# FFN up-projection: three 256-column products into the same PSUM columns in place of a 512- and a 256-column one, with no copy and addition behind them

## The reference, cut to what matters

```
u = rms_norm_2(h, norm2_gain[l])
up = causal_depthwise_conv(u @ ffn_up_w[l].astype(dt), ffn_conv_w[l], ffn_conv_b[l])
a_branch, v_branch = jnp.split(up, 2, axis=-1)
h = h + (jax.nn.gelu(a_branch) * v_branch) @ ffn_down_w[l].astype(dt)
```

## Time and profile before

| what | us |
|---|---|
| median of 3 runs | 1531.29 |
| lowest and highest run | 1531.23, 1532.5 |
| span of the profiled execution | 1529.9 |
| TensorE busy in that span | 1484.0 |
| up stage, tiles 3 to 47 | 127.25 |

### The profile page before, as it was taken

The page is one execution under the profiler, slowest core; times in us unless marked ns, Lnnn a source line. Parts: engine busy times, 40 slices in busy tenths (PEclk is TensorE's granted clock), DMA queues, the critical chain, the costliest instruction groups (busy, mean ns, idle before and its releaser), DMA issues.

```text
span 1529.9 us, 19087 instructions
## 1 busy us (share of the span) xinstructions
PE 1484.0 (97%) x7702; PEld 877.0 (57%) x7702; DVE 544.2 (36%) x1133; ACT 456.5 (30%) x796; POOL 151.6 (10%) x124
## 2 busy tenths in 40 slices
PE   8989999999999999999999999999999999999998
PEld 6755454544444445974554544445444696788886
DVE  5645111121111113034311111211111577688965
ACT  4541111111111112453111111111111561577654
POOL 0211000000000002952100000000000530001200
PEclk9999999999999999999999999999999999999999
DMA  8655999999999999745699999999999765555410
GB/s 298 247 221 220 379 425 429 426 428 427 428 427 429 426 423 398 257 177 228 253 422 420 428 428 428 426 428 428 427 428 410 283 220 205 181 200 186 166 55 28
DMA packets 76227, 502.67 MB, mean 329 GB/s; under 512 B 4720, under 2 KB 6000, under 8 KB 49136
## 3 DMA queue, kind: packets, MB, share of 16 engines
q1 hardware_dynamic: 75280, 495.18, 79.5%
q0 software_dynamic: 864, 6.29, 1.0%
HBM read 500.40 MB, written 1.05 MB: 328 GB/s over the span
## 4 chain that ended last, share of the span: by engine, by line
PE 86%; DMA 5%; DVE 4%; ACT 2%; issue 2%; SPq 1%; POOL 1%; DVEq 0%; ACTq 0%
PE bank L969 26%; PE bank L1002 14%; PE bank L828 9%; PE bank L915 7%; PE bank L1283 6%; PE bank L793 5%; DMA ring<-in_w_up 4%; PE bank L1311 4%; PE bank L929 3%; PE bank L1285 3%; SPq L576 1%; PE bank L984 1%; PE bank L875 1%; PE bank L862 1%; PE bank L887 1%
## 5 line engine op out<-in xcount | busy, mean ns | idle before, releaser
L969 PE MATMUL bank<-ring,arena 128*64 128x512 f32 x1280 | 283.7, 599 | 8.5 <-issue 6.8
L969 PEld LDWEIGHTS bank<-ring,arena 128*64 128x64 f32 x1280 | 94.3, 138 | 192.8 <-issue 192.0
L969 PE MATMUL bank<-arena 128*64 128x512 f32 x576 | 169.9, 599 | 5.2 <-issue 5.2
L1906 DVE TENSOR_TENSOR arena<-arena,bank 128x512 f32<-128x512 f32 x32 | 22.0, 687 | 382.3 <-PE bank L969 382.3
L1002 PE MATMUL bank<-ring,arena 128*64 128x512 f32 x640 | 141.8, 595 | 2.4 <-ACT arena L1450 2.4
L1283 PE MATMUL bank<-x_split,w_high 128*128 128x512 f32 (+1 forms) x408 | 139.1, 393 | 0.2 <-DVE x_split L1731 0.2
L915 PEld LDWEIGHTS bank<-SEL,x_by_row 128*128 128x128 f32 x1024 | 116.7, 192 | 25.8 <-issue 24.3
L915 PE MATMUL bank<-SEL,x_by_row 128*128 128x128 f32 x1024 | 122.8, 278 | 0.0
L969 PEld LDWEIGHTS bank<-arena 128*64 128x64 f32 x576 | 55.9, 138 | 113.6 <-issue 113.6
L1920 DVE SCALAR_TENSOR_TENSOR y_low<-bank,ST,y_high 128x512 fp32r<-128x512 f32 x64 | 48.0, 751 | 202.4 <-ACT y_high L1454 202.4
L1454 ACT ACTIVATE y_high<-bank,ST 128x512 fp32r<-128x512 f32 x64 | 44.0, 687 | 245.6 <-PE bank L1002 245.6
(11 more groups left out here) (327 smaller groups left out, 2220.5 us busy)
## 6 DMA issues: line engine op xcount, KB each, us to landing
ring<-in_w_gate SPq DMA_DIRECT2D x32, 2048.0 KB, 27.5
ring<-in_w_up SPq DMA_DIRECT2D x32, 2048.0 KB, 23.0
ring<-in_w_down SPq DMA_DIRECT2D x32, 2048.0 KB, 24.5
arena<-in_w_gate SPq DMA_DIRECT2D x18, 2048.0 KB, 25.0
arena<-in_w_up SPq DMA_DIRECT2D x18, 2048.0 KB, 24.4
arena<-in_w_down SPq DMA_DIRECT2D x18, 2048.0 KB, 26.7
ring<-in_ffn_up SPq DMA_DIRECT2D x12, 2048.0 KB, 8.1
ring<-in_w_in SPq DMA_DIRECT2D x8, 2048.0 KB, 13.5
```

Of the source, the lines that this page charges most:

```text
L969: last = nc.tensor.matmul(bank[4 + m][64 * e:64 * e + 64, :], XG[:, c, 64 * e:64 * e + 64], w[e][:, c, :], start=(c == 0), stop=(c == C - 1))
```

## The change

For tiles 3 to 47 each of the 8 steps now issues three matmuls of 256 columns, all into the bank's columns `[0:256]`: `WHI` by `XHI`, `WHI` by `XLO`, `WLO` by `XHI`. The bank then holds the finished sum. For these tiles ScalarE's copy, VectorE's addition and their semaphore steps are gone; ScalarE's first tap and VectorE's other two read the bank itself through `up_sum(f)`. TensorE, before it writes a bank again, waits for the last tap of tile `f - 4` (`f_cv`, `ffn_conv`), where it waited for the addition (`f_sum`). Tiles 0 to 2 stay as they were.

```
-        FSUM = [cut(13312 + 256 * i, SEQ) for i in range(4)]
+        FSUM = [cut(13312 + 256 * i, SEQ) for i in range(WBUF)]
+
+        def up_sum(f):
+            return FSUM[f] if f < WBUF else bank[f % 4][:, 0:SEQ]
...
                 if f >= 4:
-                    pe.wait_ge(f_sum, f - 3)
-                up(f, 0, SEQ).then_inc(w_used, 1)
+                    pe.wait_ge(f_cv, f - 3)
+                w_high, w_low = WHI[f % WBUF], WLO[f % WBUF]
+                for c in range(C):
+                    for n, (a, b) in enumerate(((w_high, XHI), (w_high, XLO), (w_low, XHI))):
+                        last = nc.tensor.matmul(bank[f % 4][:, 0:SEQ], a[:, c, :], b[:, c, :],
+                                                start=(c == 0 and n == 0), stop=(c == C - 1 and n == 2))
+                last.then_inc(w_used, 1)
...
                     act.wait_ge(w_used, U_FFN + f + 1)
-                    if f >= 4:
-                        act.wait_ge(f_cv, f - 3)
-                    nc.scalar.copy(FSUM[f % 4], bank[f % 4][:, 0:SEQ]).then_inc(f_low, 1)
+                    if f < WBUF:
+                        nc.scalar.copy(FSUM[f], bank[f][:, 0:SEQ]).then_inc(f_low, 1)
                     high_weights(f + WBUF)
-                    act.wait_ge(f_sum, f + 1)
+                    if f < WBUF:
+                        act.wait_ge(f_sum, f + 1)
...
-                    nc.scalar.activation(CV[f % 4], FSUM[f % 4], ACT.Identity,
+                    nc.scalar.activation(CV[f % 4], up_sum(f), ACT.Identity,
...
             for f in range(FF2_T):
-                dve.wait_ge(f_low, f + 1)
-                v.tensor_tensor(FSUM[f % 4], bank[f % 4][:, SEQ:2 * SEQ], FSUM[f % 4], ALU.add).then_inc(f_sum, 1)
+                if f < WBUF:
+                    dve.wait_ge(f_low, f + 1)
+                    v.tensor_tensor(FSUM[f], bank[f][:, SEQ:2 * SEQ], FSUM[f], ALU.add).then_inc(f_sum, 1)
                 low_weights(f + WBUF)
...
-                    ins = v.scalar_tensor_tensor(CV[f % 4][:, j:SEQ], FSUM[f % 4][:, 0:SEQ - j], wj, CV[f % 4][:, j:SEQ],
+                    ins = v.scalar_tensor_tensor(CV[f % 4][:, j:SEQ], up_sum(f)[:, 0:SEQ - j], wj, CV[f % 4][:, j:SEQ],
                                                  ALU.mult, ALU.add)
```

## The result

| | before | after |
|---|---|---|
| median, us | 1530.69 (20 runs) | 1533.78 (20 runs) |
| ratio, 95% interval | | 1.0021, 1.0014 to 1.0028 |
| span of the profiled execution | 1529.9 | 1531.5 |
| tiles 3 to 47 of the up stage | 127.25 | 129.65 |
| from the start of the down stage to the end of the span | 73.2 | 73.2 |

The runs before were taken again beside those after; the ratio is made from them. The changed kernel is slower by 0.21%, 3.2 us by the ratio with an interval from 2.1 to 4.3. The forecast of 1533.7 us meets the time, but to the last tenth only by luck: its base, the median of three runs, was 0.6 us too high (1531.29 against 1530.69), and the 2.4 us that it added were 0.7 less than the 3.1 us between the medians. It gave 74% to a change within 0.2% and 23% to a greater loss.

What follows compares the result with a forecast made beforehand. TensorE, busy 97% of the span, was taken as the bound. Its new pace added 2.35 us, 2.4 with the first step's loss, all else 0: 1531.29 + 2.4 = 1533.7 us, range 1531.6 to 1535.4.

Steps and rivals of the forecast that it cites:

- The new pace: Up stage, tiles 3 to 47: three matmuls a step take 0.3600 us as on line L828, +2.35 us in all.
- The old pace: Up stage, tiles 3 to 47, before the change: 0.3535 us a step, 127.25 us for 360 steps.
- The sum of 4.8 us: Up stage: cost of the change if an old step took 0.347 us; excluded from the range.
- The reason given for 0.3535: Old long matmul reads two halves of x_split and writes two bank halves, costing some 0.0065 us a step.
- Copy and addition: ScalarE's copy and VectorE's addition, removed 45 times, run beside TensorE's work: worth 0 us on the path.
- Taps from PSUM: VectorE's taps reading the bank: about 0.455 us each, against 0.50 for half a pair before; cost 0.
- The moved wait: TensorE's wait at a tile's head for taps four tiles earlier: 2.87 us of room at tile 4, cost 0.
- VectorE's relief: Up stage, second half: without the addition VectorE needs 2.54 us a tile, not 2.88; late weights less likely, no time gained.
- The new beat: Up stage, second half: VectorE, needing 2.54 us a tile, gets pauses beside TensorE's 2.88 us a tile.
- Loads that don't hide: Second weight load of each step exposed: up to +26 us, 1557 us (4%), or all loads in the open, 1600 us (1%).
- A cheap second load: Repeated load of the same high weights nearly free: step 0.353 us or below, 1531.3 to 1528.9 us; chance 8%.
- A moved wait that bites: TensorE waits at each tile for slow taps: with 0.2 us more a tile, +9 us on top, 1543 us; chance 4%.

Runs made afterwards that it cites:

- e8_both: Kernel before, with low and high FFN inputs side by side and the low-weight product sent to columns [256:512]: stage 127.25 us, ratio 0.9996.
- e2_behind_only: Kernel before with its old products, but copy and addition gone, taps reading one half of the bank, TensorE waiting for taps: stage 127.25 us, ratio 1.0011.
- e5_three_two_places: Kernel before with three 256-column matmuls a step, high by high into [256:512], the others into [0:256], copy and addition kept: stage 129.6 us.
- e7_wait_two_earlier: Changed kernel, but TensorE waits for the taps of tile f - 2 instead of f - 4: span 1552.6 us, stage 150.6 us.
- e6_six_of_128: Changed kernel with every product cut into two 128-column matmuls, six a step: span 1643.2 us, stage 241.2 us.

## Why the prediction was right, and which term was too small

**The new pace, 0.3600 us a step.** Right to the third digit: 0.3601. It was read from a place of the same program that has the same shapes and order, and that reading held in every profile that has the new form: 129.65, 129.63 and 129.6 us.

**The old pace, 0.3535 us a step.** This is the term that was mis-sized. The number is right for the execution that was profiled, and wrong as the kernel's pace: of nine profiles of the old form six have 127.25 us and three 124.87. Three of the nine are of the kernel before itself, and one of these is fast. Against the slower pace the changed kernel loses 2.40 us. Against the faster one it loses 129.65 + 66.87 - 124.87 - 67.53 = 4.1 us, since it doesn't wait for VectorE in the down stage (66.87 is its down stage). At six to three the mean is 3.0 us, 0.195%; this is an estimate, and the share of a third comes from nine profiles and is rough. The measured loss is 0.21%, 0.14 to 0.28. That interval holds the 3.0 us, but also the 2.4 of the forecast (0.16%), so the times don't show that the second pace made the difference. Where the stage begins varies more than that: from 1328.44 to 1330.92 us in the nine profiles.

**The sum of 4.8 us, set aside.** The prediction worked out that at 0.347 an old step would make the change cost +4.8 us, and wrote that this is no end of its range, "the measured old pace holds". It was the other end, for executions at the faster pace. With the 0.7 us given back it is 4.1.

**The reason given for 0.3535,** two halves of `x_split` read and two of a bank written, fell: with both made simple (`e8_both`) the pace was 0.3535 again, and without either edit it was 0.347 once.

**Copy and addition: 0 us.** Right, by `e2_behind_only`: without them, 127.25, and by `e5_three_two_places`: with them, 129.6. **Taps from PSUM: 0.** Right; 0.99 us a pair as from SBUF, where the line between two rows gave 0.455 each, 0.91 a pair. **The moved wait: 0.** Right, and `e7_wait_two_earlier` shows how it would have looked.

**VectorE's relief.** The direction was right, and so was its worth of nothing. The down stage lasts 66.87 us from first to last start in the changed kernel, and the same in `e5_three_two_places`, which keeps the copy and the addition. So the wait of 0.7 us that the old form has at its faster pace goes with TensorE's longer step, not with VectorE's relief. The new beat was foreseen; that most of the low weights would also become up to 0.48 us cheaper was not.

**The rivals.** Loads that don't hide are out at a step of 0.3601 us, though `e6_six_of_128` shows how near their floor is. The rule of the Trainium skill, "TensorE: Matmul & The Clock Gate", section "What overlaps and what doesn't", that a load overlaps running matmuls only when the row groups differ, would have made it 1600 us; the trace disagrees, with loads of 0.192 us and matmuls that start 0.120 us apart on the same rows. A cheap second load would have left the step at 0.353 us or below, and is out by the same 0.3601. A moved wait that bites would show in TensorE's waits, as in `e7_wait_two_earlier`, and the changed kernel has none.

## What to carry to other kernels

Where a stage belongs to TensorE, a change that streams the same columns in more matmuls costs time, and what it takes off other engines is worth nothing until they are late. Here the third matmul of a step cost 0.0067 us against the slower old pace and 0.0133 against the faster, as long as it had 256 columns. Cut to 128 columns, each added matmul cost (241.2 - 129.65) / 1080 = 0.103 us. The pace of a new form is best read where the same program already has it. A pace from one profile is one draw: before a loss of a tenth of a per cent is summed from it, the profile of the unchanged kernel should be taken two or three times.

## What the runs showed of the hardware that was not expected

- One and the same stream of alternating 512- and 256-column matmuls, each with its weight load, ran at 0.3535 us a step in six executions and at 0.347 in three, at the same granted clock. Threes of 256 columns had one pace only: the two stretches of the earlier trace rows lasted 46.07 to 46.08 and 23.03 to 23.04 us in all fourteen profiles.
- A stream of 128-column matmuls, each with a load of 128 columns, runs at 0.1117 us a matmul, hardly faster than one of 256 columns at 0.120.
- VectorE's 1024-element subtraction takes 1.23 us alone, and longer where GpSimd's product is already running when it starts. The added time is the overlap less 0.15 us. With 0.14 us of overlap, in most tiles of the changed kernel, nothing is added. With 0.28 it took 1.36 (changed kernel, 1451.0), with 0.63 it took 1.71 (kernel before), and with 0.73 it took 1.81 (`e2_behind_only`). Twice in `e2_behind_only` VectorE started first, by 0.04 and 0.05 us. Then its subtraction took 1.23, and GpSimd's product 1.78 and 1.79 in place of 0.74. So in these traces the one that starts second pays.
- This is why the low weights became cheaper. In the kernel before, the product starts during the addition (at 1427.18, for 0.74 us, beside the earlier trace rows) and runs into the subtraction. In the changed kernel nearly all of it falls into VectorE's pause; in the last eight tiles in which it runs, it reaches further into the subtraction, which then takes 1.27 to 1.36 us. The removed addition isn't needed for it: `e5_three_two_places` keeps the addition, and its subtraction takes 1.25 us where I read it, at 1440.25. GpSimd's row of the changed kernel, to be held against VectorE's pause from 1430.13 to 1430.88:

```profile
1430.28 0.74 POOL L717 TENSOR_TENSOR arena<-arena 128x256 f32<-128x256 f32 x1 [2.14 <-DVE arena L2286]
```
